# A state space layer whose product sums move from TensorE to GpSimd, whose scans become long, and whose turned-back states are added in pairs on VectorE

## The reference, cut to what matters

```python
dt = jnp.exp(log_dt)[:, None]
mag = jnp.exp(lr * dt)
a_re, a_im = mag * jnp.cos(li * dt), mag * jnp.sin(li * dt)      # one complex a for each group and state
bu_re = jnp.einsum('bsgc,gpc->bsgp', u, bb_re)                   # inputs of the states, bu_im alike
h = associative_scan(complex_linear_combine, (a, bu), axis=1)    # h[s] = a * h[s-1] + bu[s]
y = jnp.einsum('bsgp,gcp->bsgc', h_re, c_re) - jnp.einsum('bsgp,gcp->bsgc', h_im, c_im)
y = jax.nn.gelu(y + d_skip * u)
```

## Time and profile before

| | |
|---|---|
| median of 3 runs | 3222.91 us (3220.38 to 3223.18) |
| the profiled execution: its own time | 3220.77 us |
| its span | 3219.0 us |
| PE busy, share of the span | 3145.1 us, 98% |
| DVE, ACT, POOL busy | 64%, 33%, 44% |
| the state space stage, first work to the barrier's end | 936 to about 1080 us, 4.5% of the span |

### The profile page before, as it was taken

How to read it: one execution, slowest core, us unless ns; L and a number is a source line. 1 busy time by engine, 2 the same in 40 slices (tenths; PEclk the granted TensorE clock), 3 DMA queues, 4 the chain that set the end, 5 groups by cost and what they waited for, 6 DMA issues and landing times.

```text
span 3219.0 us, 52392 instructions
## 1 busy us (share of the span) xinstructions
PE 3145.1 (98%) x19570; PEld 2742.7 (85%) x19570; DVE 2044.2 (64%) x3811; ACT 1054.8 (33%) x2049; POOL 1417.5 (44%) x1185
## 2 busy tenths in 40 slices
PE   8999999989999999999999999999999999999998
PEld 8898989979998888878888888988889888888886
DVE  4757575755679312487777775555553777777766
ACT  3545454541123211232222221544341422222221
POOL 5434344423249233665555544411104755555533
PEclk9999999999999999999999999999999999999999
DMA  7211102052101211111111111000003011111111
GB/s 196 76 55 45 60 28 69 22 190 70 50 4 21 61 41 51 66 53 52 52 52 52 52 52 62 8 20 17 14 12 105 27 53 52 52 52 52 52 51 54
DMA packets 180105, 173.35 MB, mean 54 GB/s; under 512 B 50043, under 2 KB 162875, under 8 KB 179771
## 3 DMA queue, kind: packets, MB, share of 16 engines
q1 hardware_dynamic: 179838, 170.72, 16.8%
q10 hardware_dynamic: 96, 0.26, 0.0%
HBM read 156.97 MB, written 19.23 MB: 55 GB/s over the span
## 4 chain that ended last, share of the span: by engine, by line
PE 62%; DVE 2%; ACT 1%; issue 1%; POOL 1%; POOLq 0%; DVEq 0%; ACTq 0%
PE banks L2602 16%; PE banks L78 13%; PE banks L80 13%; PE banks L79 13%; PE banks L3419 2%; PE banks L3396 1%; PE banks L214 1%; PE banks L3353 0%; PE banks L3354 0%; POOL x L182 0%; PE banks L3335 0%; PE banks L3362 0%; POOL rstd L177 0%; ACT x L198 0%; PE banks L2229 0%
## 5 line engine op out<-in xcount | busy, mean ns | idle before, releaser
L2839 DVE TENSOR_TENSOR x<-x,banks 128x512 f32<-128x512 f32 x784 | 521.8, 687 | 240.2 <-PE banks L2602 230.3
L78 PE MATMUL banks<-winbuf_hi,xt_hi 128*128 128x256 f32 x1024 | 302.5, 295 | 12.2 <-ACT qkn L920 5.4
L80 PE MATMUL banks<-winbuf_hi,xt_lo 128*128 128x256 f32 x1024 | 290.4, 284 | 0.0
L79 PE MATMUL banks<-winbuf_lo,xt_hi 128*128 128x256 f32 x1024 | 290.3, 283 | 0.0
L78 PEld LDWEIGHTS banks<-winbuf_hi,xt_hi 128*128 128x128 f32 x1024 | 196.4, 192 | 33.3 <-issue 16.0
L78 PE MATMUL banks<-h1t_hi,f1w_buf_hi 128*128 128x512 f32 x512 | 199.5, 390 | 1.6 <-issue 1.6
L78 PE MATMUL banks<-h3t_hi,f2w_buf_hi 128*128 128x512 f32 x512 | 199.4, 390 | 1.6 <-issue 1.6
L80 PE MATMUL banks<-h1t_hi,f1w_buf_lo 128*128 128x512 f32 x512 | 199.2, 389 | 0.0
L80 PE MATMUL banks<-h3t_hi,f2w_buf_lo 128*128 128x512 f32 x512 | 199.2, 389 | 0.0
L79 PE MATMUL banks<-h3t_lo,f2w_buf_hi 128*128 128x512 f32 x512 | 199.2, 389 | 0.0
L79 PE MATMUL banks<-h1t_lo,f1w_buf_hi 128*128 128x512 f32 x512 | 199.2, 389 | 0.0
(11 more groups left out here) (544 smaller groups left out, 9433.1 us busy)
## 6 DMA issues: line engine op xcount, KB each, us to landing
f1w_raw<-in_w_ff SPq DMA_DIRECT2D x32, 1024.0 KB, 5.1
f2w_raw<-in_w_ff SPq DMA_DIRECT2D x32, 1024.0 KB, 5.0
winraw<-in_w_in SPq DMA_DIRECT2D x128, 128.0 KB, 3.3
gluw_raw<-in_ssm_w_glu SPq DMA_DIRECT2D x14, 512.0 KB, 4.4
x<-in_x SPq DMA_DIRECT2D x8, 512.0 KB, 6.5
wow_raw<-in_w_out SPq DMA_DIRECT2D x4, 1024.0 KB, 6.1
x<-in_x SPq DMA_DIRECT2D x1, 4096.0 KB, 15.8
gew_raw<-in_w_ple_gate SPq DMA_DIRECT2D x4, 1024.0 KB, 4.9
```

What stands on the lines that cost most here:

```text
L78: nc.tensor.matmul(out, a.hi, b.hi, start=start, stop=False)
L79: nc.tensor.matmul(out, a.hi, b.lo, start=False, stop=False)
L80: return nc.tensor.matmul(out, a.lo, b.hi, start=False, stop=stop)
L2839: nc.vector.tensor_tensor(xx, xx, chip.ps[:, 4 + 2 * (p % 2) + g, :], ALU.add).then_inc(s_acc, 1)
```

## The change

1. `in_products` on GpSimd is three products and now two sums (L1934 of the kernel after), five instructions; `in_matrix` on TensorE is eight transposes in place of 16 matmuls, and `minus_ident` is gone. The products stand behind `out_products(b)`, for block b+2.
2. For blocks 0 and 1 they are made in the gated embedding's stage, behind GpSimd's last split: `early_products`, 13 instructions, the sums `b_sum` and the two changes of `a_powers_back` among them, which VectorE did at the stage's start. Memory for them comes from a smaller scratch area for DMA descriptors.
3. At the start TensorE does `in_matrix(0)` first, in other banks, and `chunk_states(0)` before `tokens(1)`; ScalarE's order follows.
4. The skip goes into `kernels` as two matmuls (L2018) and leaves VectorE. SP then waits for ScalarE's copy, not for VectorE.
5. Two scans of 512 elements take the place of eight of 128. They read the decay from a tile that ScalarE fills (`decays`) with a zero at each pair's first element.
6. `turned_back` adds the four `hs` in pairs, two more instructions, and `outputs` does two products in place of four.

```diff
@@ class S5
+    def early_products(self, pool):
+        tt = self.chip.nc.gpsimd.tensor_tensor
+        tt(self.ardif[:, :, :], self.apr[1][:, :, :], self.apr[0][:, :, :], ALU.subtract).then_inc(self.made, 1)
+        tt(self.bsum[:, :, :], self.bb[0][:, :, :], self.bb[1][:, :, :], ALU.add).then_inc(self.made, 1)
+        pool.wait_ge(self.made, 1)
+        tt(self.apr[1][:, :, :], self.apr[0][:, :, :], self.apr[1][:, :, :], ALU.add).then_inc(self.made, 1)
+        for e in range(2):
+            pool.wait_ge(self.made, 3 + 5 * e)
+            for n, dst in enumerate((self.first, self.early[e][1], self.early[e][0])):
+                tt(dst[:, :, :, :], *self.in_factors(n, e), ALU.mult).then_inc(self.made, 1)
+            pool.wait_ge(self.made, 3 + 5 * e + 3)
+            for dst, op in zip(self.early[e], (ALU.subtract, ALU.add)):
+                tt(dst[:, :, :, :], self.first[:, :, :, :], dst[:, :, :, :], op).then_inc(self.made, 1)
@@ stage_gated_embedding, gpsimd
             for n in range(1, chunks):
                 ws.do_split(pool, n)
+            t.early_products(pool)
@@ stage_s5, gpsimd
-            in_products(0)
             for b in range(NB):
-                if b + 1 < NB:
-                    in_products(b + 1)
                 out_products(b)
+                if b + 2 < NB:
+                    in_products(b + 2)
@@ stage_s5, tensor
                 for c in range(2):
                     for a in range(PB):
-                        out = chip.ps[:, 4 + c, a * P:(a + 1) * P]
-                        for n, by in ((0, chip.ident), ((2, minus), (1, chip.ident))[c]):
-                            last = nc.tensor.matmul(out, p[b % 2][n][:, a, :, :].rearrange("p j c -> p (j c)"),
-                                                    by[:, :], start=n == 0, stop=n != 0)
+                        last = nc.tensor.transpose(chip.ps[:, (4 if b else 0) + c, a * P:(a + 1) * P],
+                                                   src[c][:, a, :, :].rearrange("p j c -> p (j c)"), chip.ident[:, :])
@@ kernels
+                for h in range(2):
+                    skip = diag[:, b * GB:(b + 1) * GB, :].rearrange("p (a h) c -> p h a c", h=2)[:, h]
+                    out = chip.ps[0:GCH, 2 + h, :].rearrange("p (a n) -> p a n", n=P)[:, :, 0:GCH]
+                    last = nc.tensor.matmul(out, chip.ident[0:GCH, 0:GCH], skip, start=False, stop=True,
+                                            skip_group_check=True)
@@ outputs
-                    for n in range(4):
+                    for c in range(2):
                         for h in range(2):
                             rows = slice(NST * h, NST * h + NST)
-                            last = nc.tensor.matmul(outs[h], hs[n][rows, a, :],
+                            last = nc.tensor.matmul(outs[h], hs[2 * c][rows, a, :],
@@ stage_s5, scalar
+            def decays(b):
+                if b >= 2:
+                    act.wait_ge(s_sc, 2 * b - 2)
+                nc.scalar.activation(decay[b % 2][:, :, 1:NCHK], t.mag8[:, b * PB:(b + 1) * PB].unsqueeze(2).to_broadcast(
+                    [P, PB, NCHK - 1]), ACT.Copy).then_inc(s_dec, 1)
@@ scanned
-                    for a in range(PB):
-                        n = b * PB + a
-                        last = nc.vector.tensor_tensor_scan(ht[c][:, a, :], t.mag8[:, n:n + 1].to_broadcast([P, NCHK]),
-                                                            g[c][:, a, :], 0.0, ALU.mult, ALU.add)
-                    last.then_inc(s_sc, 1)
+                    nc.vector.tensor_tensor_scan(*(z[:, :, :].rearrange("p a n -> p (a n)") for z in (ht[c], decay[b % 2], g[c])),
+                                                 0.0, ALU.mult, ALU.add).then_inc(s_sc, 1)
@@ turned_back
-                dve.wait_ge(s_h, 4 * b + 4)
+                dve.wait_ge(s_h, 6 * b + 4)
+                for c in range(2):
+                    nc.vector.tensor_tensor(out[2 * c], out[2 * c], out[2 * c + 1], ALU.add).then_inc(s_h, 1)
+                dve.wait_ge(s_h, 6 * b + 6)
```

More of the change, by code:

```diff
@@ L1430, in __init__, with in_factors @@
         self.small = [at(f"brief{n}", 138 + 0.125 * n, [P, PAIRS]) for n in range(14)]
-        self.landed, = sems(chip.nc, None, "t5", "landed")
+        self.early = [[at(f"early{e}{c}", -12 + 4 * e + 2 * c, [P, S5_PB, CL, GCH]) for c in range(2)] for e in range(2)]
+        self.first = at("p_first", 102, [P, S5_PB, CL, GCH])
+        self.bsum = at("b_sum", -4, [P, PAIRS, GCH])
+        self.ardif = at("a_difference_back", -2, [P, PAIRS, CL])
+        self.landed, self.made = sems(chip.nc, None, "t5", "landed made")
+    def in_factors(self, n, b):
+        rows = slice(b * S5_PB, (b + 1) * S5_PB)
+        left, right = (self.bsum, self.bb[0], self.bb[1])[n], (self.apr[0], self.ardif, self.apr[1])[n]
+        shape = [P, S5_PB, CL, GCH]
+        return left[:, rows, :].unsqueeze(2).to_broadcast(shape), right[:, rows, :].unsqueeze(3).to_broadcast(shape)
+    def early_products(self, pool):
[11 more added lines that the diff above has]
+                tt(dst[:, :, :, :], self.first[:, :, :, :], dst[:, :, :, :], op).then_inc(self.made, 1)
     def load(self, sp, io):
```

97 lines of the change are left out of this document (52 added, 45 removed).

## The result

The changed kernel takes **3243.18 us** (median of 4 runs, 3238.18 to 3245.22), the kernel before 3222.98 (3220.38 to 3223.18): a ratio of 1.0065, 95% interval 1.0053 to 1.0076. It is slower by 20.2 us. The forecast had the sign right and the size wrong: 7.2 us were expected, and 3243 lies above the range's end of 3240. The profiled execution took 3243.5 us with a span of 3241.6, before 3219.0.

A forecast was written before the change was run, and what follows sets the result against it. VectorE and GpSimd were to bind together at 17.3 us a turn, in place of TensorE's 15.47. 3220.8 + 2.6 (layer) + 4.6 (embedding) = 3228.0, 3230 us for the median; range 3217 to 3240, own range 3226 to 3237.

The forecast's parts named there:

- TensorE leaves the bound, VectorE and GpSimd bind together: State space layer: TensorE's turn falls from 15.47 to 10.8 us; VectorE's 17.3 and GpSimd's 17.9 set the turn.
- The start: Layer's start: in_matrix(0) runs at once, so VectorE begins about 942, 10.7 us earlier.
- The pairs: VectorE's turn beside GpSimd: six instructions over hs in place of four take 9.2 us, before 6.11.
- The early wait: Layer's first turns: outputs(0) stands behind kernels(1), which waits for q; VectorE loses 4.6 us.
- The long scans at 1.1 each: VectorE's turn: two scans of 512 elements take 2.2 us beside GpSimd, where eight short ones took 2.61.
- VectorE's turn (17.3) and GpSimd's (17.9 beside it): Layer: VectorE's 5.84 + 2.2 + 9.2; GpSimd's 11.7 us of work lengthened by VectorE holding it up.
- The turns: Layer: 15.5 us lost at 1.6 a turn, in the early wait and in fewer turns without GpSimd.
- The last outputs: Layer's end: outputs behind block 7 take 4.7 us, 2.2 gained.
- TensorE's clock stays low: Rival, chance 0.13: slow clock for TensorE's whole turn, 18.5 us, above 17.3; total 3239.
- The gated embedding: Stage before the layer: 13 GpSimd instructions (13.5 us) delay VectorE's rotations by 10 us; TensorE stops for 4.6.

The follow-up runs named there:

- e11: Kernel before with one edit: VectorE adds the turned-back states in pairs and TensorE's outputs take fewer matmuls; 3235.97 us, ratio 1.0042.
- e3: Changed kernel without the sums of turned-back states in pairs, four products with them on TensorE; 3227.25 us, ratio 1.0019.
- e5: Changed kernel with eight short scans and the skip added by VectorE right ahead of them; 3243.39 us, ratio 1.0059.
- e8: Kernel before with only the skip moved from VectorE to TensorE; 3232.12 us, ratio 1.0030.
- e13: Changed kernel with the skip back on VectorE, right ahead of the two long scans; 3241.52 us, ratio 1.0063.
- e2: Changed kernel with eight short scans over the decay's column again, without ScalarE's decay tile; 3250.48 us, ratio 1.0086.
- e4: Changed kernel with idle matmuls ahead of TensorE's waits for outputs and kernels, and 20 ahead of the last outputs; 3242.79 us, ratio 1.0062.
- e9: Kernel before with only the early products of two blocks on GpSimd and the start that goes with them; 3222.24 us, ratio 1.0006.
- e12: e10 with two long scans in place of eight short ones, behind the skip on VectorE; 3217.16 us, ratio 0.9988.
- e15: e12 run once more, unchanged; 3218.27 us, ratio 0.9991.
- e10: e9 with the early products begun later, at 914.7, before the rotations end; 3218.60 us, ratio 0.9991.
- e1: Changed kernel with GpSimd's early products made to wait for the end of VectorE's rotations; 3233.9 us, ratio 1.0040.
- e6: Changed kernel with the edits of e1 and e3 together; 3225.2 us, ratio 1.0008.
- e7: e6 with the products' sums left to TensorE from the third block on; 3222.61 us, ratio 0.9998.

## Why the forecast was right in sign and wrong in size

*TensorE leaves the bound, VectorE and GpSimd bind together*: right. GpSimd waits for no one, and VectorE, behind its start, for 5.2 us only.

*The start*: right. The first `turned` came 5.5 us behind the stage's start (6 forecast); 11.1 us gained for 10.7.

*The pairs*, six instructions over `hs` at 9.2 us: 9.3 to 9.5 measured in the plain turns. Right, and this part of the change is the dearest: 15.5 us alone (e11), 15.9 in the changed kernel (e3).

*The early wait*, 4.6 for `outputs(0)` behind `kernels(1)`: the place is right. TensorE waited 6.76 for `q` (8 forecast), VectorE 2.06 for the outputs, less than half of what was forecast, since its own turn had grown.

*The long scans at 1.1 each*: right for a scan by itself (2.33 for two) and wrong beside GpSimd (4.0 to 4.5). This is the step that failed first. I took from the earlier trace rows that scans in a row keep GpSimd out and thought it a property of scans. e5, e8 and e13 show that it hangs on what VectorE issues right ahead of them, which the change takes away. The own range of the forecast allowed 1.06 a turn for it; it was 2. In a plain turn it is the whole miss: `turned` took 5.5 us (5.84 forecast), the scans 4.5 (2.2), the six instructions over `hs` 9.4 (9.2). And e13, with the scans at 2.32 and the skip back at 1.25, has plain turns of 18.4 to 18.6, which is what the forecast's own terms then add up to (5.84 + 1.25 + 2.3 + 9.2 = 18.6).

But shorter turns gave back hardly any time: e13 takes 3241.5, 1.7 less, which is inside the scatter of the changed kernel's four runs (3238.18 to 3245.22). The second mistake is one of the model, and it is in part argued. I counted VectorE's turn (17.3) and GpSimd's (17.9 beside it) from what each had cost the other in the old mixture of instructions. With no pause left on either side, GpSimd's ten instructions and VectorE's share one time, and much of what one is spared the other pays, as GpSimd's 3.8 us more in e13 and 6.2 in e5 show. The turns gave 20.9 us for 15.5.

*The last outputs*, 4.7 forecast: 9.0. The term was worked out at the full clock. The rival *TensorE's clock stays low* had the mechanism: the granted clock was 0.50, 0.69, 0.72 and 0.77 in four stretches of 10 us among the turns, where a plain turn had 1.00 before. It put the price in the wrong place, though. The half clock holds for about half of TensorE's turn, and that still fits into VectorE's (15.9 us of work from 1009.96 on, then 3.5 of waiting). What it costs is 4.3 us in the last outputs and, by the timeline, the wait of 3.14 in the seventh turn: the outputs that VectorE waits for began at 1065.18 and took until 1074.5; with the 4.7 of the full clock they would have ended before its scans did, at 1071.4 (an estimate). So the rival's 3239 came out nearer than the forecast's 3230 by luck.

*The gated embedding*, 4.6: the waits measured 4.5, at the place that was named. The size is in part luck: GpSimd's 13 instructions took 18.1 us (892.19 to 910.31) and not 13.5, the rotations ended 11.5 us later and not 10, and TensorE stopped twice and not once. What was missing is what the clock does behind the waits: 43 matmuls in a stretch of 10 us that held 86. Most kernels with the early products at the first moment have the same waits of 4.4 to 4.5 and a stage 6.2 to 6.4 us longer (e2 to e4, e9, e13), so some 2 us belong to the clock. In the profiled execution of after it is 9.2: the clock fell lower behind the waits (0.66 from 910 to 920, 0.88 in e9), and the first 10 us of the stage, ahead of the products, already ran at 0.83. A start at 0.83 is not the change's: e12 had it and took 120.9 us, e15, the same kernel without it, 119.4. The rest, about 1.3, lies in the longer half clock behind the waits, which e5 shows too; why it was longer there is open.

Added up: the embedding 4.6 over forecast, the turns 5.4, the last outputs 4.3, the rest 1.1, or 15.4 us between a span that was to grow by 7.2 and one that grew by 22.6. How the turns' 5.4 divide between the scans and the sharing is not settled: e13 makes the scans shorter, but also brings in the skip's 1.25 a turn and the wait of 2.52.

The version that came out best keeps of the change the early products, begun some 20 us before the rotations end in it, and the long scans behind the skip: 3217.16 and 3218.27 us in two groups of runs, 0.9988 (0.9979 to 0.9998) and 0.9991 (0.9982 to 1.0000). It is 3 us, hardly more than can be measured, and one of the two intervals touches 1. Why the short instruction ahead of the scans keeps GpSimd out, by its length, its 16 partitions, its place or the wait for a semaphore that goes with it, was not tried.

## What to carry to other kernels

When work is moved off an engine that is only just the bound onto two that are already full and lengthen each other's instructions, the freed time is worth nothing, and each added instruction costs its loaded length (here 1.53 us), not the one that it has alone (0.63). Then price a pause twice: by its own length, and by the slower clock behind it, above all where the next work is covered by nothing. Work put into an idle stretch of an engine can be placed so that it ends just ahead of the stage's end: as soon as possible cost 6 us here, as late as possible 4, in between 1.6.

## What the runs showed of the hardware

- Eight scans of 128 elements right behind a short VectorE instruction on 16 partitions took 2.61 us in every turn beside a busy GpSimd (before, e5, e9, e10, e11), and 3.6 to 10.4 without it (e2, e8). Two scans of 512 took 2.32 with it (e12 to e15), 4.0 to 4.7 without (after, e1, e3, e4, e6, e7).
- A scan of 512 elements takes 1.16 us alone, a product of 512 takes 0.63. The Trainium skill, "DVE: opcode table, instruction layouts, handler registers and perf-mode slots", section 6, says that the built-in scan runs at half throughput; the trace agrees.
- Keeping GpSimd out of VectorE's scans saved little where both were always busy: the scans became 2 us shorter a turn (e13), GpSimd's work 3.8 us longer in all, and the time 1.7 less.
- The 48 matmuls of the last outputs took 5.0 us right behind idle matmuls (e4) and 9.0 to 9.2 behind a wait of 2.2 to 3.1 us (after, e2, e5, e11, e13), at a granted clock near 0.5. The wait alone doesn't fix the price: behind one of 2.6 they took 6.6 in e1.
